# Splitting each weight block into its high and low part in two steps of 1024 columns

## The reference, cut to what matters

```python
for l in range(DEPTH):                                  # 2
    m = token_mixer(x, w_in[l], ...)                    # attention, conv, retention, gated, projected
    x = layer_norm(ALPHA * x + m, ln1_g[l], ln1_b[l])
    f = swiglu(...) if l % 2 == 0 else moe_swiglu(...)  # (silu(x @ w_gate) * (x @ w_up)) @ w_down
    x = layer_norm(ALPHA * x + f, ln2_g[l], ln2_b[l])
```

## Time and profile before

| what | value |
|---|---|
| median of 3 runs | 1907.62 us |
| the profiled execution's own time | 1904.11 us |
| its span | 1902.3 us |
| PE busy | 1853.1 us (97%) |
| DVE busy | 1432.6 us (75%) |
| ACT busy | 1133.7 us (60%) |
| granted TensorE clock, mean | 0.996 |

### The profile page before, as it was taken

How to read it: one execution, slowest core, us unless ns; L and a number is a source line. 1 busy time by engine, 2 the same in 40 slices (tenths; PEclk the granted TensorE clock), 3 DMA queues, 4 the chain that set the end, 5 groups by cost and what they waited for, 6 DMA issues and landing times.

```text
span 1902.3 us, 28024 instructions
## 1 busy us (share of the span) xinstructions
PE 1853.1 (97%) x11100; PEld 1613.4 (85%) x11104; DVE 1432.6 (75%) x1212; ACT 1133.7 (60%) x972; POOL 0.2 (0%) x4
## 2 busy tenths in 40 slices
PE   7999999999999999999999999999999999999996
PEld 6899998999978999996888888888888887888885
DVE  4685577544466665768889889888898888888987
ACT  5444444343436444445777777777677777777774
POOL 0000000000000000000000000000000000000000
PEclk9999999999999999999999999999999999999998
DMA  7633444554436333454998989989989899899993
GB/s 313 230 144 133 156 177 178 188 187 176 181 144 251 134 139 139 171 206 160 369 364 325 369 335 356 381 323 368 362 333 369 328 361 352 328 365 357 347 362 151
DMA packets 36026, 504.69 MB, mean 265 GB/s; under 512 B 3968, under 2 KB 4096, under 8 KB 5248
## 3 DMA queue, kind: packets, MB, share of 16 engines
q1 hardware_dynamic: 34960, 498.07, 69.5%
q10 hardware_dynamic: 1008, 5.77, 0.8%
HBM read 502.78 MB, written 1.05 MB: 265 GB/s over the span
## 4 chain that ended last, share of the span: by engine, by line
PE 79%; DVE 7%; DMA 7%; ACT 4%; issue 3%; SPq 0%; DVEq 0%; ACTq 0%
PE PS L345 14%; PE PS L347 13%; PE PS L346 13%; PE PS L331 11%; PE PS L333 10%; PE PS L332 10%; DMA raw<-wstream 7%; DVE w_lo L1117 4%; ACT w_hi L828 3%; PE PS L715 1%; PE PS L741 1%; PE PS L483 1%; PE PS L515 1%; PE PS L498 1%; PE PS L784 0%
## 5 line engine op out<-in xcount | busy, mean ns | idle before, releaser
L1117 DVE TENSOR_TENSOR w_lo<-raw,w_hi 128x2048 fp32r<-128x2048 f32 x472 | 1077.1, 2290 | 322.7 <-ACT w_hi L828 320.8
L828 ACT ACTIVATE w_hi<-raw 128x2048 fp32r<-128x2048 f32 x472 | 901.9, 1915 | 343.7 <-PE PS L347 181.2
L331 PE MATMUL PS<-xT_hi,w_hi 128*128 128x256 f32 x1456 | 419.1, 288 | 7.0 <-DVE w_lo L1117 6.1
L332 PE MATMUL PS<-xT_lo,w_hi 128*128 128x256 f32 x1456 | 412.3, 283 | 0.0
L333 PE MATMUL PS<-xT_hi,w_lo 128*128 128x256 f32 x1456 | 412.2, 283 | 0.0
L345 PE MATMUL PS<-w_hi,xT_hi 128*128 128x512 f32 x896 | 355.1, 396 | 2.6 <-DVE xT_lo L1556 1.5
L347 PE MATMUL PS<-w_hi,xT_lo 128*128 128x512 f32 x896 | 349.6, 390 | 0.0
L346 PE MATMUL PS<-w_lo,xT_hi 128*128 128x512 f32 x896 | 349.0, 390 | 0.0
L331 PEld LDWEIGHTS PS<-xT_hi,w_hi 128*128 128x128 f32 x1456 | 279.5, 192 | 18.8 <-issue 14.5
L332 PEld LDWEIGHTS PS<-xT_lo,w_hi 128*128 128x128 f32 x1456 | 279.7, 192 | 0.2
L333 PEld LDWEIGHTS PS<-xT_hi,w_lo 128*128 128x128 f32 x1456 | 279.5, 192 | 0.0
(11 more groups left out here) (246 smaller groups left out, 1326.6 us busy)
## 6 DMA issues: line engine op xcount, KB each, us to landing
raw<-wstream SPq DMA_DIRECT2D x236, 2048.0 KB, 8.8
soft<-ln ACTq DMA_DIRECT2D x4, 1024.0 KB, 6.3
X<-x SPq DMA_DIRECT2D x1, 1024.0 KB, 4.9
out<-X ACTq DMA_DIRECT2D x2, 512.0 KB, 2.7
cst<-consts SPq DMA_DIRECT2D x1, 906.0 KB, 11.0
sm<-small SPq DMA_DIRECT2D x1, 729.0 KB, 12.7
bufA<-router ACTq DMA_DIRECT2D x1, 512.0 KB, 3.4
rg<-constb SPq DMA_DIRECT2D x1, 335.0 KB, 11.4
```

What stands on the lines that cost most here:

```text
L331: mm(o, wh, rhs_hi[:, k, :], start=(k == 0), stop=False)
L332: mm(o, wh, rhs_lo[:, k, :], start=False, stop=False)
L828: activate(w_hi[:, at % RING], raw_half(at // 2 % RING, at % 2), ACT.Copy).then_inc(hi_done, 1)
L1117: v.tensor_tensor(w_lo[:, at % RING], raw_half(at // 2 % RING, at % 2), w_hi[:, at % RING], ALU.subtract).then_inc(lo_done, 1)
```

## The change

The copy on ACT and the subtraction on DVE are each cut in two instructions of 1024 columns. A new semaphore `half_done` tells DVE that the first 1024 columns of `w_hi` are there. `hi_done` is signalled by the second step of ACT, `lo_done` by the second of DVE, and all other waits stay.

```diff
-        hi_done, lo_done = sem("hi_done"), sem("lo_done")
+        half_done, hi_done, lo_done = sem("half_done"), sem("hi_done"), sem("lo_done")
...
-                activate(w_hi[:, at % RING], raw_half(at // 2 % RING, at % 2), ACT.Copy).then_inc(hi_done, 1)
+                src = raw_half(at // 2 % RING, at % 2)
+                activate(w_hi[:, at % RING, 0:SUB // 2], src[:, 0:SUB // 2], ACT.Copy).then_inc(half_done, 1)
+                activate(w_hi[:, at % RING, SUB // 2:SUB], src[:, SUB // 2:SUB], ACT.Copy).then_inc(hi_done, 1)
...
+                src = raw_half(at // 2 % RING, at % 2)
+                dve.wait_ge(half_done, k * 6 + (at + 1))
+                v.tensor_tensor(w_lo[:, at % RING, 0:SUB // 2], src[:, 0:SUB // 2], w_hi[:, at % RING, 0:SUB // 2],
+                                ALU.subtract)
                 dve.wait_ge(hi_done, k * 6 + (at + 1))
-                v.tensor_tensor(w_lo[:, at % RING], raw_half(at // 2 % RING, at % 2), w_hi[:, at % RING],
-                                ALU.subtract).then_inc(lo_done, 1)
+                v.tensor_tensor(w_lo[:, at % RING, SUB // 2:SUB], src[:, SUB // 2:SUB],
+                                w_hi[:, at % RING, SUB // 2:SUB], ALU.subtract).then_inc(lo_done, 1)
```

## The result

| kernel | median us | runs | range |
|---|---|---|---|
| before | 1906.89 | 4 | 1902.20 to 1909.39 |
| changed | 1887.14 | 4 | 1886.73 to 1887.51 |

The ratio is 0.9897 with a 95% interval of [0.9881, 0.9912]: 19.7 us faster. The profiled execution took 1886.94 us, its span 1885.1 instead of 1902.3.

A forecast was written before the change was run, and what follows sets the result against it. PE, busy 97% of the span, was taken as the bound. Gains of 0.8 + 1.2 + 2.4 + 4.9 + 0.8 - 0.3 = 9.8 us, from 1907.6, gave about 1898 us, range 1894 to 1903.

The forecast's parts named there:

- A split's cost: Each split: ready after 3.46 us instead of 4.24, 0.78 sooner; holds DVE 2.28 instead of 2.20 us.
- Compress subs: Short stretch bound by DVE: the last sub PE waits for is 0.62 us sooner; two layers, 1.2 us.
- Change of items: Between expert items: PE's whole 0.30 us pause goes, at eight places; 2.4 us gained.
- Start: PE's first product: the halves end at 14.35 instead of 15.12; 0.8 us gained.
- Late tiles: Experts, ten PE waits for hT_lo: seven gain 4.9 us, three behind gathers lose 0.3.
- SyncE: Tile requests: sooner as places free sooner, at most 2 us over the kernel from late tiles; taken as nothing.
- Elsewhere nothing: Mixer and dense part: splits lie far ahead of PE, delays of 0.1 us each hidden beside matmuls; no change.
- End: Behind the last expert: L1597 starts at about 1883.5 instead of 1884.28; 0.8 us gained.
- Rival 1: Experts: gain given back to the transfers, whose landing does not move; 2.8 us remain, 1904.8 us; chance 0.16.
- rival 2: Experts: DVE becomes the bound, from 2.65 us a split; slower, for example about 1938 us; chance 0.05.
- rival 3: Whole kernel: the cut does nothing PE sees, the counted pauses being chance; 1905 to 1908 us; chance 0.05.
- Rival 4: Experts: earlier requests remove all hT_lo pauses and short ones; 14 to 17 us, 1891 to 1894 us; chance 0.12.

The follow-up runs named there:

- e3: Changed kernel, but SyncE learns of a free place through a 256-element GpSimd addition, so tiles are requested 0.96 us later in the mean; 1890.78 us.
- e5: Kernel before, but each tile is loaded in two 1 MB transfers, each requested when its own sub's place is free; 1892.17 us.
- e1: Kernel before with the two-step split in the expert stage alone; 1889.60 us against 1906.27.
- e2: Kernel before with DVE's subtraction cut in two steps that both follow ACT's whole copy, so no overlap; 1910.48 us against 1906.27.
- e8: Changed kernel with the split in eight steps of 256 columns instead of two; 1934.17 us.
- e11: Changed kernel with a longer GpSimd addition (576 elements) ahead of each tile request, which comes 1.7 us later in the mean; 1949.30 us.
- e4: Kernel before, with requests delayed through a 256-element GpSimd addition, 1.07 us later in the mean; 1927.88 us.
- e7: Changed kernel with the split in four steps of 512 columns instead of two; 1890.21 us.

## Why the prediction was off

The mechanism was right and the sum too small. What failed is the term of the late tiles, together with two effects that it had at nothing: that the tiles themselves land sooner, and that a pause costs PE more than its length. Point by point:

- *A split's cost.* Ready 0.78 us sooner: measured 4.25 and 3.46 (medians), 0.79. Steps 1.13 to 1.15 apart on DVE and 0.95 to 0.97 on ACT, as taken. By the full drain of the Trainium skill (VectorE: DVE Perf Modes, "The DRAIN you can't avoid") it would have been 0.70. The same section also says that a next op that is not held starts earlier, and that is the case here: the two steps at 1579.76 start 1.14 apart at 1.23 and 1.22 us.
- *Compress subs.* Right: from the first wait to the last 11.22 us before and 10.63 now in layer 0, 0.59 (predicted 0.62), and 0.60 in layer 1.
- *Change of items, 2.4 us.* Right, all eight pauses went (2.4 us).
- *Start, 0.8 us.* PE starts 0.83 sooner (14.44 against 15.27), as reckoned, but 0.61 of it is lost by 19 us, to the clock. That is chance between two executions, as far as the runs show (last section).
- *Late tiles, 4.9 - 0.3: the term that failed.* Laid side by side matmul by matmul, the 14.4 us of expert stage are: 2.4 at the changes of items, 5.7 in seven long pauses for `hT_lo` (0.42 to 1.18 each), 1.2 in five short ones (0.18 to 0.27), 1.8 in four pauses before gathers, 2.9 in slower matmuls behind the pauses, 0.4 elsewhere. The seven long ones were sized about right: 0.79 us less for each, and at most its whole length, comes to 4.9 of their 5.7. The five short ones I gave nothing. At the gathers I had a loss of 0.3, and they gained 1.8. There the subtraction is not in the way, since L1570 waits for L1043 behind ACT's copy; this copy takes 0.1 longer, as predicted, but its tile has landed sooner (lines below). That is the "SyncE" step, which I put at nothing with a bound of 2 us. Measured, the tile is free 0.73 us sooner and lands 0.48 sooner after the same start (16.70 to 16.23). What I missed is that the split and the request draw on one reserve (e3 to e5), so that the late tiles nearly end rather than get 0.79 us shorter. How much of the long and short pauses went by the shorter split alone stays open, since no run separates it: in e3 too the tiles land sooner than before.
- *A pause costs more than its length.* The matmuls of the 5 us behind the twenty pauses (eight, seven and five, 9.3 us) came 2.9 us late in all over the usual distance, 0.15 us for each pause. At 1030.50 the next start was 1030.84, 0.34 us away, and then 0.24 several times instead of 0.23. I left that out.
- *Elsewhere nothing.* Nearly right in sum, but not in its parts. In the mixers and norms PE's pauses grew by about a microsecond, at L498 from 0.76 to 1.10 and at the norm after layer 0 from 1.56 to 1.83; at other places of these stages PE gained some 0.9, so 0.2 is lost in all. At L498 the longer hold of DVE is enough for it: its waits are 1.2 us in before and e1, 1.5 in e2, where ACT's copy is whole, and 1.6 with the change.
- *End, 0.8 us.* Right (2.37 to 1.59), and 0.8 more came with it, by the clock.
- *Carry-over.* I added the 3.5 us between the profiled execution and the median to the forecast. They are probably pauses of other executions, which went too: before ranges over 7 us, the changed kernel over 0.8. No profile of another execution shows it.
- *A sign that did not come.* DVE's idle time behind ACT was to fall by over 200 us; it fell by 86 (320.8 to 235.1). DVE's idle time in all could fall only by what DVE got busier and the span shorter, 31 and 17 us.

The place of the earlier trace rows with the change, ACT and then DVE, where the idle time before `hT_lo` is 0.42 us and was 0.77:

```profile
1117.87 1.07 ACT L829 ACTIVATE w_hi<-raw 128x1024 fp32r<-128x1024 f32 x1 [1.66 <-DMA raw<-wstream]
...
1120.39 0.69 DVE L1576 TENSOR_TENSOR act_lo<-PS,act_hi 128x512 fp32r<-128x512 f32 x1 [0.42 <-ACT act_hi L1045]
```

In the span: 1.25 us before the experts, 14.4 in them, 1.55 after them, 17.2 in all. Rival 1 (given back to the transfers) is refuted by e1 and e5, rival 2 by e8, which shows where it would begin; rival 3 by the interval. Rival 4 comes nearest: all but two of the pauses of `hT_lo` went, and the short ones with them, but its 14 to 17 us were too small, and its cause, earlier requests, is only half of it (e3).

## What to carry to other kernels

Where three engines and a transfer queue hand a ring around, add up the whole way around (request, landing, each step until the place is free) and lay it beside the time that the bound engine needs for as many pieces: with a reserve of about one microsecond in 17.6, a split shorter by 0.8 us or a load by halves removed nearly all pauses, and requests later by 1.07 cost the kernel before 21.6. Count pauses by the distance of matmul starts, with what the restart costs, and give the sooner landing a term of its own. When an experiment delays something by work on another engine, look whether that work slows the engines beside it (e11). A cut into steps pays as long as the engine with the most steps stays below the bound's pace: here two steps, with four already no better and eight beyond it.

## What the runs showed of the hardware that was not expected

**The lower clock at the start ends at different times.** PE's first products of 256 columns come 0.21 us apart, 1.2 columns a nanosecond, and then 0.12. In the kernel before the distance changes at 18.3 us:

```profile
17.97 0.41 PE L331 MATMUL PS<-xT_hi,w_hi 128*128 128x256 f32 x1
18.18 0.33 PE L332 MATMUL PS<-xT_lo,w_hi 128*128 128x256 f32 x1
18.35 0.28 PE L333 MATMUL PS<-xT_hi,w_lo 128*128 128x256 f32 x1
18.47 0.28 PE L331 MATMUL PS<-xT_hi,w_hi 128*128 128x256 f32 x1
```

In the changed kernel, whose products begin 0.83 us sooner, it changes at about 18.9:

```profile
14.44 0.55 PE L331 MATMUL PS<-xT_hi,w_hi 128*128 128x256 f32 x1 [4.79 <-DVE w_lo L1123]
...
18.42 0.41 PE L331 MATMUL PS<-xT_hi,w_hi 128*128 128x256 f32 x1
18.63 0.39 PE L332 MATMUL PS<-xT_lo,w_hi 128*128 128x256 f32 x1
18.85 0.29 PE L333 MATMUL PS<-xT_hi,w_lo 128*128 128x256 f32 x1
```

So the lower level (1.2 GHz) lasted longer here, and 0.22 us of the 0.83 was left. The granted clock reads 1.00 there in both profiles, so the level is read from the distances; in e3, where it is recorded, it reads 0.50 from 16 to 18 us at the same distance. That the earlier start is the cause is not shown. In the thirteen profiles PE starts at 14.0 to 15.3 us and the distance changes at 17.8 (e11) to 21.3 us (e4): at 17.8 to 20.3 in those that start before 14.6, at 18.4 to 21.3 in the others.

At the end the shorter wait did bring something. Behind the wait for L1597 the scatter's matmuls started 0.40 to 0.43 us apart before and 0.23 apart now. The granted clock fell to 0.50 within a microsecond of the scatter's start in five of the six profiles where PE waited 2.2 or 2.3 us there (not in e5), and in none of the seven where it waited 1.4.

**Short dips.** In e7 the window around 67 us has a granted clock of 0.91, and so has the one around 617 in e3; both profiles lose about 1.5 us there. The window of e7:

```profile
58.00:76.00 18.00, 16.38 (x128) 15.01 (x126) 8.34 (x19) 11.08 (x28) 0.00 (x0) 0.91 0.46 176
```

Ahead of the dip two starts of PE lay 1.02 us apart, at 60.90. e8 has two dips, behind distances of 1.39 us, and e11 has five in the experts, each 0.3 to 1.4 us behind a distance of 2.2 to 3.0 us. Here is a window within one of them, where PE's starts are 0.43 us apart:

```profile
1530.00:1533.00 3.00, 3.00 (x9) 2.35 (x8) 2.82 (x4) 0.00 (x0) 0.00 (x0) 0.50 1.02 437
```

Not each such pause is followed by a dip: in e11 those at 1056.79 (2.22 us) and 1186.56 (2.12) are not. What decides it was not tried, and the other half of e7's loss ahead of the experts stays open as well.

**Landing gets quicker when the request comes later.** With 0.96 us more of request delay in e3 the time from issue to landing fell from 9.34 to 8.37 us. The tile before is then nearer its end: at a request it still had 3.5 us to go in the changed kernel, 2.5 in e3. Within one profile of the kernel before, tiles that are requested with under 2 us of the tile before to go land after 7.8 us, those with over 4 after 9.9. So a delay or an advance of a request reaches the landing only in part.

**An addition on GpSimd and a subtraction on DVE slow each other.** In e11 (its lines above), where they overlap, 1.14 us became up to 5.47 on GpSimd, and 1.21 up to 2.2 on DVE.
